# Weights times [high | low] activations as one 512-column matmul in six feed-forward stages

## The reference, cut to what matters

```python
def sq_relu_mlp(h, w_up, w_down):                 # first block, D_FF = 4096, both layers
    return jnp.square(jax.nn.relu(h @ w_up)) @ w_down

def conv_ffn(h, w_up, conv_w, w_down):            # second block, D_FF_2 = 2816, both layers
    up = causal_dwconv(h @ w_up, conv_w)
    a, u = up[..., :D_FF_2], up[..., D_FF_2:]
    return (jax.nn.silu(a) * u) @ w_down

x = x + sq_relu_mlp(rms_norm(x, norm_ffn_g[layer]), ffn_w_up[layer], ffn_w_down[layer])
x = x + conv_ffn(rmsnorm(x, norm_ffn_g[i]), ffn_w_up[i], ffn_conv_w[i], ffn_w_down[i])
```

## Time and profile before

| | |
|---|---|
| median of 3 runs | 1151.09 us (1150.94 to 1151.53) |
| the profiled execution | 1150.85 us, span 1149.1 us |
| mean granted TensorE clock | 0.998 of full speed |
| TensorE matmul / weight load busy | 99% / 96% of the span |
| VectorE / ScalarE / GpSimd busy | 75% / 57% / 23% |
| HBM | 203.5 MB moved, 177 GB/s mean |

### The profile page before, as it was taken

How to read it: one execution, slowest core, us unless ns; L and a number is a source line. 1 busy time by engine, 2 the same in 40 slices (tenths; PEclk the granted TensorE clock), 3 DMA queues, 4 the chain that set the end, 5 groups by cost and what they waited for, 6 DMA issues and landing times.

```text
span 1149.1 us, 26243 instructions
## 1 busy us (share of the span) xinstructions
PE 1132.5 (99%) x9706; PEld 1106.8 (96%) x9706; DVE 863.3 (75%) x1387; ACT 652.6 (57%) x1075; POOL 267.2 (23%) x256
## 2 busy tenths in 40 slices
PE   9999999999999999999999999999999999999997
PEld 8998999999997999999999999999999999999997
DVE  6876877656696777755587589999867788999854
ACT  6666566545446656644556466666555455666543
POOL 0001500012230600011110163444421025454421
PEclk9999999999999999999999999999999999999999
DMA  9642655655643465565454345555566655565461
GB/s 302 209 147 87 208 187 188 209 184 183 165 142 107 153 214 185 181 205 197 148 175 156 111 147 184 183 196 173 174 197 214 216 186 184 185 200 191 148 204 60
DMA packets 213136, 203.51 MB, mean 177 GB/s; under 512 B 11840, under 2 KB 212800, under 8 KB 213072
## 3 DMA queue, kind: packets, MB, share of 16 engines
q1 hardware_dynamic: 212928, 202.44, 55.1%
q10 hardware_dynamic: 144, 0.20, 0.1%
HBM read 201.57 MB, written 1.05 MB: 176 GB/s over the span
## 4 chain that ended last, share of the span: by engine, by line
PE 94%; DVE 3%; ACT 2%; issue 1%; DMA 0%; POOL 0%; DVEq 0%; ACTq 0%; SPq 0%; POOLq 0%
PE gemm L713 28%; PE gemm L715 28%; PE gemm L714 28%; PE gemm L724 2%; PE gemm L725 1%; PE gemm L726 1%; DVE w_lo L1610 1%; PE score L906 1%; PE score L1025 1%; DMA x<-in_xT 0%; ACT w_hi L1238 0%; PE misc L751 0%; PE score L1028 0%; ACT act_a L1256 0%; PE score L1128 0%
## 5 line engine op out<-in xcount | busy, mean ns | idle before, releaser
L1610 DVE TENSOR_TENSOR w_lo<-w_raw,w_hi 128x1024 fp32r<-128x1024 f32 (+2 forms) x404 | 481.0, 1195 | 150.1 <-ACT w_hi L1238 148.3
L1238 ACT CAST w_hi<-w_raw 128x1024 fp32r<-128x1024 f32 (+2 forms) x404 | 402.0, 1001 | 152.6 <-PE gemm L715 145.1
L713 PE MATMUL gemm<-act_a,w_hi 128*128 128x256 f32 (+1 forms) x1704 | 472.6, 277 | 1.9 <-DVE w_lo L1610 1.0
L714 PE MATMUL gemm<-act_a,w_hi 128*128 128x256 f32 (+1 forms) x1704 | 469.1, 275 | 0.0
L715 PE MATMUL gemm<-act_a,w_lo 128*128 128x256 f32 (+1 forms) x1704 | 469.1, 275 | 0.0
L713 PEld LDWEIGHTS gemm<-act_a,w_hi 128*128 128x128 f32 (+1 forms) x1704 | 318.3, 187 | 7.1 <-DVE w_lo L1610 3.3
L714 PEld LDWEIGHTS gemm<-act_a,w_hi 128*128 128x128 f32 (+1 forms) x1704 | 318.5, 187 | 0.4
L715 PEld LDWEIGHTS gemm<-act_a,w_lo 128*128 128x128 f32 (+1 forms) x1704 | 318.3, 187 | 0.3
L713 PE MATMUL gemm<-hid,w_hi 128*128 128x256 f32 x864 | 238.1, 276 | 0.0
L715 PE MATMUL gemm<-hid,w_lo 128*128 128x256 f32 x864 | 237.7, 275 | 0.0
L714 PE MATMUL gemm<-hid,w_hi 128*128 128x256 f32 x864 | 237.7, 275 | 0.0
(11 more groups left out here) (273 smaller groups left out, 1388.7 us busy)
## 6 DMA issues: line engine op xcount, KB each, us to landing
w_raw<-in_ffn_w_up SPq DMA_DIRECT2D x76, 1024.0 KB, 5.2
w_raw<-in_ffn_w_down SPq DMA_DIRECT2D x32, 1024.0 KB, 5.0
w_raw<-in_gla_w_in SPq DMA_DIRECT2D x12, 1024.0 KB, 5.3
w_raw<-in_ffn_w_down SPq DMA_DIRECT2D x16, 768.0 KB, 4.2
w_raw<-in_sc_w_in SPq DMA_DIRECT2D x12, 1024.0 KB, 5.1
w_raw<-in_fox_w_in SPq DMA_DIRECT2D x10, 1024.0 KB, 6.8
w_raw<-in_ffn_w_down SPq DMA_DIRECT2D x16, 640.0 KB, 3.9
w_raw<-in_fox_w_out SPq DMA_DIRECT2D x4, 1024.0 KB, 4.9
```

The source lines that it names most:

```text
L713: nc.tensor.matmul(ps, wh[:, k, cols], act[:, k0 + k, 0, :], start=start and k == 0, stop=False)
L714: nc.tensor.matmul(ps, wh[:, k, cols], act[:, k0 + k, 1, :], start=False, stop=False)
L1238: nc.scalar.copy(split_half(w_hi, nc_, nj), raw_half(nc_, nj)).then_inc(w_hi_ready, 1)
L1610: nc.vector.tensor_tensor(split_half(w_lo, nc_, nj), raw_half(nc_, nj), split_half(w_hi, nc_, nj).bitcast(F32), ALU.subtract).then_inc(w_l ...
```

## The change

In the six stages the matmuls of a k-step become two: the high weights against high and low activations side by side (512 columns, a whole bank), and the low weights against the high activations (into the bank's first 256 columns). Afterwards the bank's first half holds high x high + low x high, the second half high x low; the eviction adds the halves. `m_act` gets the address 240 modulo 256 bytes. The semaphore `act_evac` is renamed `plain_evac`.

```diff
-        m_act = split_tiles("m_act", 5, past=192)
+        m_act = split_tiles("m_act", 5, past=240)
...
+            def wide_block(ps, c, j, act, k0=0, start=True, stop=True, tiles=None):
+
+                wh, wl = split_half(w_hi, c, j), split_half(w_lo, c, j)
+                nk = kind_of(c)[1]
+                for k in range(nk):
+                    if tiles is not None:
+                        pe.wait_ge(act_ready, tiles + k + 1)
+                    both = act[:, k0 + k, :, :].rearrange("p s t -> p (s t)")
+                    nc.tensor.matmul(ps[:], wh[:, k, :], both, start=start and k == 0, stop=False)
+                    last = nc.tensor.matmul(ps[:, 0:T], wl[:, k, :], act[:, k0 + k, 0, :], start=False, stop=stop and k == nk - 1)
+                return last
...  # up, TensorE (down and conv_down call wide_block in the same way, on hid)
-                        pe.wait_ge(act_evac, AE[stage] + n - 3 + 8 * i)
-                        feature_block(gemm[b][:, 0:T], c, j, act_a, tiles=tiles if n == 0 else None).then_inc(half_done, 1)
+                        pe.wait_ge(plain_evac, AE[stage] + n - 3 + 8 * i)
+                        wide_block(gemm[b], c, j, act_a, tiles=tiles if n == 0 else None).then_inc(half_done, 1)
...  # up, ScalarE
-                        nc.scalar.activation(tmp[:, n % 4, :], bank_of(stage, n)[:, 0:T], ACT.Relu).then_inc(act_evac, 1)
+                        nc.scalar.copy(tmp[:, n % 4, :], bank_of(stage, n)[:, T:2 * T]).then_inc(up_low, 1)
...  # down, ScalarE
                             prep(C0[stage] + cc, j, (i, 4, 2))
+                            if cc == 3:
+                                act.wait_ge(half_done, halves_before(C0[stage] + cc, j, (i, 4, 2)) + 1)
+                                nc.scalar.copy(tmp[:, j, :], bank_of(stage, j)[:, T:2 * T]).then_inc(down_low, 1)
...  # up, VectorE
-                        dve.wait_ge(act_evac, AE[stage] + n + 1 + 8 * i)
-                        nc.vector.tensor_tensor(tmp2[:, n % 4, :], tmp[:, n % 4, :], tmp[:, n % 4, :],
-                                                ALU.mult).then_inc(sq_ready, 1)
+                        dve.wait_ge(half_done, halves_before(C0[stage] + n // 2, n % 2, (i, 4, 8)) + 1)
+                        ps = bank_of(stage, n)
+                        dve.wait_ge(up_low, SQ[stage] + n + 1 + 8 * i)
+                        nc.vector.tensor_tensor(tmp[:, n % 4, :], ps[:, 0:T], tmp[:, n % 4, :], ALU.add).then_inc(plain_evac, 1)
+                        dve.wait_ge(plain_evac, AE[stage] + n + 1 + 8 * i)
+                        nc.vector.scalar_tensor_tensor(out=tmp2[:, n % 4, :], in0=tmp[:, n % 4, :], scalar=0.0, in1=tmp[:, n % 4, :],
+                                                       op0=ALU.max, op1=ALU.mult).then_inc(sq_ready, 1)
...  # down, VectorE
-                                nc.vector.tensor_tensor(tmp[:, j, :], bank_of(stage, j)[:, 0:T], rstd_of(norm_name)[:, 0:T],
-                                                        ALU.mult).then_inc(dve_evac, 1)
+                                ps = bank_of(stage, j)
+                                dve.wait_ge(down_low, RT[stage] + j + 1 + 2 * i)
+                                nc.vector.tensor_tensor(tmp[:, j, :], ps[:, 0:T], tmp[:, j, :], ALU.add).then_inc(dve_evac, 1)
                                 dve.wait_ge(dve_evac, DE[stage] + j + 1 + 2 * i)
+                                nc.vector.tensor_tensor(tmp[:, j, :], tmp[:, j, :], rstd_of(norm_name)[:, 0:T],
+                                                        ALU.mult).then_inc(down_scaled, 1)
+                                dve.wait_ge(down_scaled, RT[stage] + j + 1 + 2 * i)
                                 t = ds(2 * i + j, 1)
                                 nc.vector.tensor_tensor(x[:, t, :], x[:, t, :], tmp[:, j, :], ALU.add).then_inc(resid_ready, 1)
...  # conv_down, VectorE
-                            ps = bank_of(stage, j)[:, 0:T]
-                            nc.vector.tensor_tensor(xt, ps, xt, ALU.add).then_inc(dve_evac, 1)
+                            ps = bank_of(stage, j)
+                            nc.vector.tensor_tensor(xt, ps[:, T:2 * T], xt, ALU.add).then_inc(first_half_added, 1)
+                            dve.wait_ge(first_half_added, FH[stage] + j + 1 + 2 * i)
+                            nc.vector.tensor_tensor(xt, ps[:, 0:T], xt, ALU.add).then_inc(dve_evac, 1)
```

More of the change, by code:

```diff
@@ L287, in build @@
         half_done = sem("half_done")
-        act_evac = sem("act_evac")
+        plain_evac = sem("plain_evac")
         dve_evac = sem("dve_evac")
         resid_ready = sem("resid_ready")
+        down_scaled = sem("down_scaled")
+        up_low = sem("up_low")
+        down_low = sem("down_low")
+        first_half_added = sem("first_half_added")
         act_hi_ready = sem("act_hi_ready")
@@ L372, in build @@
         SQ = {"U0": 0, "U1": 32}
+        FH = {"CD0": 0, "CD1": 8}
         TURN = {}
@@ L790, in up @@
                             pe.wait_ge(*before[b])
-                        pe.wait_ge(act_evac, AE[stage] + n - 3 + 8 * i)
-                        feature_block(gemm[b][:, 0:T], c, j, act_a, tiles=tiles if n == 0 else None).then_inc(half_done, 1)
+                        pe.wait_ge(plain_evac, AE[stage] + n - 3 + 8 * i)
+                        wide_block(gemm[b], c, j, act_a, tiles=tiles if n == 0 else None).then_inc(half_done, 1)
                 for b in range(4):
-                    freed[(b0 + b) % 4] = (act_evac, AE[stage] + 28 + b + 1)
+                    freed[(b0 + b) % 4] = (plain_evac, AE[stage] + 28 + b + 1)
                 stat(norm)
@@ L809, in down @@
                                 pe.wait_ge(dve_evac, DE[stage] + j - 1 + 2 * i)
-                            feature_block(gemm[b][:, 0:T], c, j, hid, k0=8 * cc,
+                            wide_block(gemm[b], c, j, hid, k0=8 * cc,
                                           start=cc == 0, stop=cc == 3,
@@ L852, in body @@
                             pe.wait_ge(dve_evac, DE[stage] + j - 1 + 2 * i)
-                        feature_block(gemm[b][:, 0:T], c, j, hid, k0=k0,
+                        wide_block(gemm[b], c, j, hid, k0=k0,
                                       start=cc % 4 == 0, stop=cc % 4 == 3,
@@ L918, in fox_pv @@
                 if h % 4 == 0:
-                    pe.wait_ge(act_evac, AE["FV"] + 2 * (h // 4) + 2)
+                    pe.wait_ge(plain_evac, AE["FV"] + 2 * (h // 4) + 2)
                 if h % 2 == 0:
@@ L935, in _ @@
                     split_ready(c, j)
-                    ps = take_bank(stage, n, (dve_evac, DE[stage] + n + 1) if s else (act_evac, AE["FQA"] + 1))
+                    ps = take_bank(stage, n, (dve_evac, DE[stage] + n + 1) if s else (plain_evac, AE["FQA"] + 1))
                     last = feature_block(ps[:, 0:T], c, j, act_a, tiles=AT["x"] if s == 0 else None)
@@ L939, in _ @@
                 elif s < 24:
-                    token_half("FV", s - 16, act_a, act_evac, AE["FV"])
+                    token_half("FV", s - 16, act_a, plain_evac, AE["FV"])
                 if s == 2:
@@ L998, in v_half @@
                 for t in range(TT):
-                    ps = take_bank("VB", 2 * j + t, (act_evac, AE["VB"] + 2 * j + t + 1))
+                    ps = take_bank("VB", 2 * j + t, (plain_evac, AE["VB"] + 2 * j + t + 1))
                     last = token_block(ps[:], lambda k: wh[:, k, :], lambda k: wl[:, k, :], t, m_act[:, 0:2])
@@ L1035, in mla_pv @@
                 if h == 0:
-                    pe.wait_ge(act_evac, AE["VB"] + 4)
+                    pe.wait_ge(plain_evac, AE["VB"] + 4)
                 ps = take_bank("MPV", h, (act_ready, AT["mctx"] + h + 1))
@@ L1122, in gla_states @@
                 pe.wait_ge(gla_act, 9)
-                pe.wait_ge(act_evac, AE["GV"] + 8)
+                pe.wait_ge(plain_evac, AE["GV"] + 8)
                 pe.wait_ge(gla_dve, 11 if chunks[0] == 0 else 15)
@@ L1171, in _ @@
             for n in range(8):
-                token_half("GV", n, act_a, act_evac, AE["GV"])
+                token_half("GV", n, act_a, plain_evac, AE["GV"])
                 if n == 0:
@@ L1203, in _ @@
                 g, part = n // 6, (n % 6) // 2
-                done = (act_evac, AE["SI"] + 2 * g + j + 1) if part == 0 else (dve_evac, DE["SI"] + 4 * g + 2 * (part - 1) + j + 1)
+                done = (plain_evac, AE["SI"] + 2 * g + j + 1) if part == 0 else (dve_evac, DE["SI"] + 4 * g + 2 * (part - 1) + j + 1)
                 ps = take_bank("SI", n, done)
@@ L1419, in _ @@
                     act.wait_ge(half_done, 1)
-                    nc.scalar.copy(f_q[:, 0, :], bank_of("FQA", 0)[:, 0:T]).then_inc(act_evac, 1)
+                    nc.scalar.copy(f_q[:, 0, :], bank_of("FQA", 0)[:, 0:T]).then_inc(plain_evac, 1)
                     root("mix0")
@@ L1439, in _ @@
                         nc.scalar.activation(f_v[:, t, g * CW:(g + 1) * CW], bank_of("FV", 2 * g + t)[:, 0:CW], ACT.Copy,
```

(12 more changed lines are left out.)

## The result

The changed kernel takes 1175.13 us (median of 4 runs, 1173.62 to 1175.39) against 1151.11 for the kernel before (1150.94 to 1151.53): a ratio of 1.0203, interval 1.0190 to 1.0215. It is 2% slower. The forecast was 1146.5, with a range from 1144 to 1163.5, so direction and range were both wrong.

What follows compares the result with a forecast made beforehand. TensorE, busy 99% of the span, was taken as the bound. Matmuls -7.8, evictions +1.98, +0.98 and +0.58, and `m_act` -0.3 sum to -4.6 us: median 1146.5 us, range 1144 to 1163.5.

Steps and rivals of the forecast that it cites:

- the first term: Matmuls of the six changed stages: each wide one saves 5.7 ns over two narrow, 1,376 k-steps, -7.8 us.
- The second reading of the earlier trace: Wide matmuls: second 256 columns cost 113.5 ns, so nothing is saved; 1154.3 us as a rival, chance 0.20.
- out of step: Rival: alternating wide and narrow matmuls never find the 113.3 ns step; 1162.6 us, or 1169.0 with both slow; chance 0.21.
- The sentence for it: Support for lost step: matmuls on `m_act` stay at 118 ns over 35 matmuls, against 113.3 for tiles at 240.
- The one against it: Argument against lost step in the changed stages: weight loads would start as now, with the matmul before; no size.
- What bounds the kernel: Whole kernel: TensorE, busy 99% of the span; weight loads do not set the 113.3 ns matmul spacing.
- The evictions: Longer evictions in the changed stages: hidden inside stages, showing at stage ends, +1.98, +0.98 and +0.58 us.
- `up` at 0: Evictions in U0 and U1: the longer chain fits under 2.67 us of matmuls with 0.1 us to spare, cost 0.
- D1: Second `down` stage: at its end, before the gate stage, ScalarE's copy and a VectorE step add +0.99 us.
- D0: First `down` stage: at its end, before KVQ, ScalarE's copy and a VectorE step add +0.99 us.
- CD0: First `conv_down` stage: at its end, the first add delays the next split and a second add follows, +0.98 us.
- CD1's tail: End of the second `conv_down` stage: nothing lies behind it, the second add costs +0.58 us.

Runs made afterwards that it cites:

- experiment 1: Probe computing nothing of the reference: streams of narrow and wide matmuls at 16 moving-tile addresses, other engines idle; wide k-step 353.3 ns at 240, narrow 340.0.
- experiment 2: Changed kernel with each 512-column matmul split into two of 256, new evictions kept: 1155.37 us, ratio 1.0033 to the kernel before.
- experiment 4: Kernel before with only `m_act` moved from 192 to 240 modulo 256 bytes: 1151.02 us, ratio 0.9998.
- the grouped one: Changed kernel with all wide matmuls of a half first, then its low-weight ones: 1168.92 us, ratio 1.0155 to the kernel before.
- experiment 7: Changed kernel with `hid` at 128 instead of 240 modulo 256 bytes: 1169.36 us, ratio 1.0154 to the kernel before.

## Why the prediction was wrong

**The step that failed** is the first term, "I take the saving of the earlier trace rows: a wide matmul of activations at 226.7 - 5.7 = 221 ns". It measured 234.5, and the narrow one behind it 118.8: +18.3 us in place of -7.8. The term had the wrong sign for two reasons that the runs separate. First, the 6.7 ns are not a cost of starting an instruction: alone at this address, 512 columns take 231.1 ns, more than two narrow matmuls (experiment 1). The second reading of the earlier trace rows, that the loss goes with the columns, was nearer, and I gave it the smaller chance. Second, alternating widths costs more on top, 353.3 against 231.1 + 113.3 = 344.4 ns. So of the 13.3 ns a k-step some 4.4 go with the columns and 8.9 with the mixing. That both come from the width, and not from the evictions, experiment 2 shows.

**The rival that came true** is "out of step". Its harder price, both kinds out of step at 350.7 ns, was 1169.0 us; the k-step took 353.3 ns (+3.6 us over 1,376), and the clock falls came on top: 1169.0 + 3.6 + 3.0 = 1175.6, where 1175.1 was measured. I gave it 0.21 and cut the range through its middle, so its harder form was left out. The sentence for it ("never leaves 118 over 35 matmuls") pointed the right way. The one against it, that loads start with the matmul before as now, says nothing of the addresses: with loads in the same order the probe's narrow k-step goes from 340 ns to between 351 and 358 when only the weights' address changes (experiment 1).

**What bounds the kernel** held: TensorE throughout, and no DMA on the path. That a narrow matmul's spacing does not depend on the size of the weight load held at this address: 113.3 ns with 16, 32 and 128 weight columns.

**The evictions** held in sum: 3.54 forecast, some 2.9 found by stages and 2.8 to 3.0 by experiment 2. The parts held less well. `up` at 0 was right, each start within 0.13 us of the forecast. D1 was 0.86 and D0 1.2, each forecast at 0.99: "GpSimd's sums of squares move by the same step and add nothing" failed at D0, where they ran beside VectorE's new multiply and it took 0.45 us longer. CD0 was 0.98 forecast and 0.37 found: before, the weight split behind the first addition waited 0.19 us for its cast and took 1.58 us beside GpSimd; now it follows without a wait and takes 1.22, which takes up most of the delay. CD1's tail was 0.46 against 0.58.

**`m_act`**, -0.3, can't be resolved in the times; the traces of experiment 4 show -0.05.

**Not foreseen:** the granted clock. Two falls of 3.41 us to the 1.2 GHz level, 1.4 to 1.5 us each, and 0.5 us in the tail. Their cause is open. The first comes right behind the longer waits at D0's end, but the split kernel has the same waits and, in its trace, only the second fall, the grouped one only the first; and the second has no wait ahead of it. Before has executions at 1152.3 us with a lower mean clock beside those at 1151.0, so it seems to have such a fall at times too; none of them has a trace.

**Still open:** what in the read of the moving operand makes the pattern. Many steady spacings are multiples of 6.67 ns, sixteen columns at 2.4 GHz: the best narrow k-step is 51 of them (48 of columns, 3 lost), the wide one at 128 and at 240 is 52 and 53, a narrow matmul 17 or 18, the best wide one alone 34. Some widths between fit too: 304 columns 140.0 ns (19 and 2), 480 columns 213.3 (30 and 2), 464 also 213.3 (29 and 3). Others don't, such as 288 columns at 134.2 ns or 512 at 231.1. That one group in sixteen is lost at least, and more by how widths and addresses fall together, describes the numbers measured; no run shows the mechanism. Open too is why CD0 and CD1 kept 353.3 ns in experiment 7.

## What to carry to other kernels

A stream of equal matmuls can sit in a step that a mix of widths never finds: before merging matmuls to save their starts, measure the very mix, at the very addresses, in a probe of a few dozen instructions. Here it gave the kernel's 353.3 ns exactly; at another address it was right for two stages and wrong for two, so check the probe by stage and not by the total, where a clock fall can make up the difference. A saving read from rows at another address is a comparison of two other places; if the same rows can be read with the other sign, the forecast's range must hold that sign whole. When comparing two times a few us apart, count the falls of the granted clock in both traces first. And a new VectorE instruction has to be priced beside what GpSimd does at that moment.

## What the hardware showed unexpectedly

- An fp32r matmul of this chip takes 113.3 ns at best for 256 columns (120.0 at another address) and 226.7 to 231.6 for 512; bf16 takes 109.2 and 215.8. bf16 with its moving columns 4 bytes apart is back at 113.3 and 225 to 227.
- 340 ns for three 256-column fp32r matmuls is the least over 256 pairs of addresses, found at 25 of them, among them all 16 with the activations 192 bytes past the weights modulo 256; the worst pair takes 368.8.
- 464 and 480 columns take the same 213.3 ns.
- A change between fp32r and bf16 inside a k-step makes it 353 to 367 ns, also at the two addresses where fp32r alone takes 340.
- The same VectorE multiply took 0.43 us twelve times with GpSimd idle beside it and 0.88 us four times with GpSimd adding.
- The granted clock fell to half once without a wait of TensorE ahead of the fall.
